# Turning 104 blocks of 128 by 128 on VectorE and by DMA instead of on TensorE, in a fused two-layer kernel on one core

## The chip, the core and the metric

The kernel runs on one core of one Trainium2 chip. The metric is the device time of one execution in microseconds (us), from the program's start to its end. TensorE (PE) multiplies matrices, VectorE (DVE) and ScalarE (ACT) work elementwise, GpSimd (POOL) does small jobs, SyncE (SP) issues almost all DMAs. PEld is TensorE's loading of the stationary operand.

## The reference, cut to what matters

Batch 1, 256 tokens, model width 2048, all in float32. Two layers follow each other.

```python
# layer 1 (first_block): proj = rms_norm(x) @ w_in          (10240 columns)
# differential attention on 4 heads, neighbourhood attention on 8 heads
mixed = g_a * (oa @ w_branch_a) + g_b * (on @ w_branch_b)
y = mixed @ w_out                       # x = x + rms_norm(y)
u = square(relu(rms_norm(x) @ w_up))    # x = x + rms_norm(u @ w_down)
# layer 2 (second_block): proj = rmsnorm(h) @ w_in_2
qk = silu(causal_dwconv(concat([ml_q, ml_k])))            # along the tokens
h_a = mlstm_chunkwise(q, k, v, i, f)
f_b = lb + (1 - lb) * sigmoid(hg_f); logf = log(f_b)      # cumulative sums along the tokens
h_b = hgrn2_chunkwise(q_b, k_b, logf, i_b)
h = h + concat([y_a, y_b]) @ w_out_2
gate = sigmoid(rmsnorm(h) @ w_pg_2);  h = h + gate * (p @ w_pe_2)
out = rmsnorm(h)
```

## The kernel before

Every large product runs as float32 split in two: a weight chunk of 512 rows by 512 columns (1 MB, four blocks of 128 rows) is loaded by SP into one of three `RAW` buffers, ACT rounds it into `HI` (`high`, L521), DVE subtracts to get `LO` (`low`, L936), and PE does three matmuls for each of the 4 row blocks and of the 2 token tiles, so 24 matmuls of 128x512 for a chunk. The activations, turned so that the contracted dimension lies on the partitions, are split in the same way into `ATH` and `ATL`.

There are 342 chunks, numbered by n in a list that every engine walks in the same order, with its own waits: 0 to 79 layer 1's `w_in`, 80 to 95 the two branches ("a", "b"), from `N_WO` = 96 `w_out`, from `N_UP` = 112 `w_up`, from `N_DN` = 176 `w_down`, from `N_IN2` = 240 layer 2's `w_in_2`, from `N_RES` = 308 `w_out_2` with `w_pe`, from `N_PG` = 326 `w_pg`. At step n ACT and DVE split chunk n+2, SP loads further ahead. `high(n)` waits until PE is done with chunk n-3, and SP's load of a chunk waits for DVE's `low` of the chunk three before it. Chunks 256 to 267 (the kind "nq") are narrower, 344 columns, so a step of PE is shorter there. Layer 2's `w_in_2` comes in the order hf (chunks 240 to 247), qk (248 to 255), nq (256 to 267), hv, vm, go, z, g.

The dictionary `side` (filled by `beside(n, name, ...)`) puts small steps behind the products of chunk n, in each engine's program: the convolution (`conv`, DVE), the forget gates (`prep`), the gate scans (`gate`), the attention steps (`da`, `na`), the recurrences (`hg`, `ml`). `behind[n]` and `before[n, t]` do this for the `unit` steps, which bring four turned blocks (group g of a product's input, token tile t) into `ATH` and `ATL`: "heads", "mix" (the gated sum `MX`), "r1", "r2", "y" and "pg" (the residual `XS` in front of `w_pg`).

Turning is done in two ways. (1) On PE: `tr` (L1478) is a matmul against the identity that gives a turned 128 by 128 block in PSUM; four of them are one step of `turned`. It serves `unit` (mix, r1, r2, y, pg), `to_heads` (layer 2's heads hf, qk, hq: PE turns 4 blocks for each token tile, ACT copies them from PSUM into `HB`, `QKR`, `HQ`), `ut` (the first up block) and the attention's `da turn`, `da back`, `na turn`. (2) On DVE and by DMA, used for the eight groups of layer 1's rope and hd heads: `turn(j)` (L1030) turns 128x512 in blocks of 32 by 32 for both token tiles; before the load of chunk m+6 (m is the step of the turn, in `turns_of`) SP waits for it and issues 8 DMAs of 64 KB from SBUF into a DRAM buffer `turned_rows[j]`, which put the blocks in their places; before the load of chunk m+7 SP waits until they have landed and loads the 512 KB back as heads ("heads", j).

Of the kernel before, what the change touches and what calls it, by code (L numbers as in the profile page):

```python
# [15 lines left out]
P = 128  # L16
D = 2048
S = 256
# [51 lines left out]
def program(nc, x, xt, w_in, w_a, w_b, w_out, w_up, w_down, w_in2, w_out2, w_pg, w_pe, p2,  # L70
            cols, lamv, rpb, rows, bif, cos_c, sin_c, nam_c, id_c, lvl_c, caus_c, out):
    with ExitStack() as ctx:
# [43 lines left out]
        def loaded(*name):  # L116
            if name not in s_ld:
                s_ld[name] = Count(sem("s_load_" + "_".join(map(str, name))), 16)
                counts.append(s_ld[name])
            return s_ld[name]  # L120
# [165 lines left out]
        for j, n in turns_of.items():  # L286
            beside(n, "turn", j)
# [9 lines left out]
        for t in range(2):  # L297
            beside(N_UP + 5 + t, "ut", 0, t)
        for j in range(1, 16):
            beside(N_UP + 4 * j + 4, "ut", j, 1)  # L300
        for i in range(3):
            beside(172 + i, "cut", i)
            beside(228 + i, "weigh", i)
        for j in range(2):
# [5 lines left out]
        for n, i in ((244, 0), (249, 1), (250, 2), (251, 3), (252, 4), (253, 5), (254, 6)):  # L310
            beside(n, "prep", i)
        for i in range(9):
            beside(257 + i, "conv", i)
# [3 lines left out]
        for i in range(3):  # L317
            beside(268 + i, "gate", i)
# [9 lines left out]
        beside(316, "p_parts")  # L328

# [9 lines left out]
        fill_early("mix", N_WO - 4, [(N_WO + 2, 1), (N_WO + 3, 0)])  # L339
        fill_early("y", N_RES - 4, [(N_RES + 2, 0), (N_RES + 2, 1)])  # L340
# [6 lines left out]
        def turned_to(j, t):  # L347

            return TURNED[(2 * (j if j < 4 else j - 2) + t) % 8]

        def heads_of(j):
            z = (QT, QT, KT, KT, None, None, QN, QN, KN, KN)[j]
            return z[:, 4 * (j % 2):4 * (j % 2) + 4, :]
# [10 lines left out]
        turned_rows = {j: nc.dram_tensor(f"turned{j}", (512, S), F32, kind="Internal").ap() for j in turns_of}  # L364
# [88 lines left out]
        def gpsimd(e):  # L453
# [15 lines left out]
            for n in range(N_ALL):  # L469
# [24 lines left out]
                if n == 266:  # L494
                    po.wait_ge(s_pe, "qk", 1, 1)
                    po.wait_ge(s_pool, LAST)
                    e.memset(VM[:, :, :, S:S + 1], 1.0).then_inc(s_pool.on("ones"))
# [6 lines left out]
        def scalar(e):  # L504
# [18 lines left out]
            def unit(name, g, t):  # L523
# [10 lines left out]
                elif name == "mix":  # L534
                    ac.wait_ge(s_pe, "unit", name, g, t)
                    ac.wait_ge(s_prod, "products", taken(name, g), t)
                    src = cut4(mis[:, place.get((name, g, t), 0), :])
# [10 lines left out]
            def cut(i):  # L548
                if i >= 64:
                    return  # L550
                ac.wait_ge(s_act, "ut", i % 16, 1)
# [3 lines left out]

            def to_heads(dst, g0, t, *name):
                ac.wait_ge(s_pe, *name)
                act(dst[:, g0:g0 + 4, t * P:(t + 1) * P], cut4(mis[:, place.get(name, 0), :]), ACT.Copy).then_inc(
                    s_act.on(*name))
# [65 lines left out]
            def ut(j, t):  # L625
                if j == 0:
                    ac.wait_ge(s_pe, "ut", 0, t)
                    act(UT[:, 0:4, t * P:(t + 1) * P], cut4(acc[:, 2 * (number["wo", 3] % 2) + t, :]), ACT.Square).then_inc(
                        s_act.on("ut", 0, t))
                else:  # L630
                    ac.wait_ge(s_dve, "up rows", j)
                    act(UT[:, 4 * j:4 * j + 4, :], UX[j % 2], ACT.Square).then_inc(s_act.on("ut", j, 1))
# [10 lines left out]
            def prep(i):  # L643
                if i == 0:
                    ac.wait_ge(s_dve, "lb")
                    act(ST[:, 16:32], ST[:, 16:32], ACT.Exp).then_inc(s_act.on("lb exp"))
                if i == 1:
                    ac.wait_ge(s_act, "hf", 1, 1)
                    act(HK, HB, ACT.Sigmoid, scale=-1.0).then_inc(s_act.on("hk"))
                if i == 2:  # L650
                    act(HB, HB, ACT.Sigmoid).then_inc(s_act.on("hb sig"))
                if i == 5:
                    ac.wait_ge(s_dve, "hb max")
                    act(HB, HB, ACT.Ln).then_inc(s_act.on("hb ln"))
# [85 lines left out]
            def evac(b):  # L740
# [6 lines left out]
                for t in range(2):  # L747
# [23 lines left out]
                    if kind == "up":  # L771
                        ac.wait_ge(s_pool, "r1")
                        act(US[:, t, :], ps[t], ACT.Relu, scale=ST[:, 52 + t:53 + t]).then_inc(s_act.on("evac", b, t))
                    if kind in ("nq", "hf", "qk", "hv", "vm", "go"):
                        ac.wait_ge(s_pool, "r2")
                    if kind == "nq":
                        act(NQ[:, t, 344 * j:344 * j + 344], ps[t], ACT.Copy, scale=RS[t]).then_inc(s_act.on("evac", b, t))
                    if kind == "hf":
                        if j:
                            ac.wait_ge(s_pe, "hf", 0, t)  # L780
# [3 lines left out]
                    if kind == "hv":  # L784
                        ac.wait_ge(s_pe, "qk", 1, 1)
                        act(HV[:, t, cols_], ps[t], ACT.Copy, scale=RS[t]).then_inc(s_act.on("evac", b, t))
                    if kind == "vm":
                        act(VM[:, t, 2 * j:2 * j + 2, 0:S], ps[t].rearrange("p (h c) -> p h c", h=2), ACT.Copy, scale=RS[t]).then_inc(s_act.on("evac", b, t))
                    if kind == "go":
                        ac.wait_ge(s_pe, "hq", 3)  # L790
# [50 lines left out]
            do = dict(lam=lam, da=da, na=na, sig=sig, ut=ut, rb=rb, cut=cut, prep=prep, conv=conv, gate=gate,  # L841
                      turn_v=turn_v, hg=hg, ml=ml, p_parts=p_parts)

            def beside_products(n):
                for name, *i in side.get(n, ()):
                    if name == "hf":
                        to_heads(HB, 4 * i[0], i[1], "hf", *i)
                    elif name == "qk":
                        to_heads(QKR, 4 * i[0], i[1], "qk", *i)
                    elif name == "hq":  # L850
                        to_heads(HQ, 4 * (i[0] // 2), i[0] % 2, "hq", *i)
                    elif name in do:
# [56 lines left out]
        def vector(e):  # L909
# [38 lines left out]
            def unit(name, g, t):  # L948
                if name in SCALE:
                    z = cut4(stage(name, g, t))  # L950
                    c0 = SCALE[name] + 4 * g
                    dv.wait_ge(s_pe, "unit", name, g, t)
                    dv.wait_ge(loaded("col"), "col")
                    tt(z, cut4(mis[:, place.get((name, g, t), 0), :]),
                       COL[:, c0:c0 + 4].unsqueeze(2).broadcast_to([P, 4, P]), ALU.mult).then_inc(s_dve.on("unit", name, g, t))

            def unit_low(name, g, t):
# [3 lines left out]
                elif name == "mix":  # L961
                    src = cut4(mis[:, place.get((name, g, t), 0), :])
# [58 lines left out]
            def turn(j):  # L1021
                if j == 0:
                    dv.wait_ge(s_pe, "x sums")
                if j >= 6:
                    dv.wait_ge(loaded("blocks", j - 6), "blocks", j - 6)
                for t in range(2):
                    if j >= 6:
                        dv.wait_ge(s_act, "evac", number["hd", j], t)
                    then()
                    e.transpose(turned_to(j, t), R[t]).then_inc(s_dve.on("turned", j, t))  # L1030
# [35 lines left out]
            def prep(i):  # L1066
                if i == 0:
                    a0, a1 = COL[:, C_LB:C_LB + 8], COL[:, C_LB + 8:C_LB + 16]
                    dv.wait_ge(loaded("col"), "col")
                    tt(LB, a0, a1, ALU.max).then_inc(s_dve.on())  # L1070
                    tt(LM, a1, LB, ALU.subtract).then_inc(s_dve.on())
                    tt(LB, a0, LB, ALU.subtract).then_inc(s_dve.on("lb"))
                    dv.wait_ge(s_act, "lb exp")
                    tt(LM, LB, LM, ALU.add).then_inc(s_dve.on())
                    then()
                    e.reciprocal(LM, LM).then_inc(s_dve.on())
                    tt(LB, LB, LM, ALU.mult).then_inc(s_dve.on())
                    ts(LM, LB, -1.0, 1.0, ALU.mult, ALU.add).then_inc(s_dve.on())
                if i in (3, 4):
                    dv.wait_ge(s_act, "hb sig")  # L1080
                    for h in range(4 * (i - 3), 4 * (i - 3) + 4):
                        ts(HB[:, h, :], HB[:, h, :], LM[:, h:h + 1], LB[:, h:h + 1], ALU.mult, ALU.add).then_inc(s_dve.on())
                        ts(HK[:, h, :], HK[:, h, :], LM[:, h:h + 1], None, ALU.mult).then_inc(s_dve.on())
                if i == 5:
                    ts(HB, HB, 1e-19, None, ALU.max).then_inc(s_dve.on("hb max"))
                if i == 6:
                    dv.wait_ge(s_act, "hb ln")
                    for h in range(8):
# [3 lines left out]
            def conv(i):  # L1092
                if i < 8:
                    x_, y_ = QKR[:, i, :], QK[:, i, :]
                    cw = lambda k: COL[:, C_CW + 8 * k + i:C_CW + 8 * k + i + 1]
                    dv.wait_ge(s_act, "qk", 1, 1)
# [32 lines left out]
            def hg(q, i):  # L1129
# [57 lines left out]
                if i == 1:  # L1187
                    dv.wait_ge(s_act, "hg edge", q)
                    tt(HP[:, :, 0:P], HW_[:, :, 0:P], k_[:, :, 0:P], ALU.mult).then_inc(s_dve.on())
                    dv.wait_ge(s_act, "hq", 3)  # L1190
# [209 lines left out]
            do = dict(lam=lam, turn=turn, da=da, na=na, cut=cut, weigh=weigh, prep=prep, conv=conv, gate=gate, hg=hg, ml_logs=ml_logs, ml=ml, ya=ya,  # L1400
# [70 lines left out]
        def tensor(e):  # L1471
# [30 lines left out]
            def unit(name, g, t):  # L1502
                if name in ("heads", "x"):
# [51 lines left out]
            def columns(n):  # L1555
# [6 lines left out]
                if k == 0:  # L1562
# [3 lines left out]
                    elif block == 2:  # L1566
                        for t in range(2):
                            pe.wait_ge(s_act, "ut", 0, t)
# [29 lines left out]

            def ut(j, t):
                if j:  # L1600
                    return
                z = acc[:, 2 * (number["wo", 3] % 2) + t, :]
                pe.wait_ge(s_act, "rb")
                pe.wait_ge(s_dve, "evac", number["wo", 3], t)
                pe.wait_ge(s_act, "evac", number["up", 0], t)
                for c in range(4):
                    r = tr(z[:, c * P:(c + 1) * P], US[:, t, c * P:(c + 1) * P])
                r.then_inc(s_pe.on("ut", 0, t))
# [27 lines left out]
            def da(u):  # L1636
# [13 lines left out]
                if 0 <= u - 1 < 8:  # L1650
# [273 lines left out]
```

## Time and profile before

| | us |
|---|---|
| median of 3 runs | 1970.18 (1970.17 to 1970.8) |
| the profiled execution's own time | 1971.09 |
| its span, first to last instruction | 1969.1 |
| granted TensorE clock over the span | 0.999 |

A page shows one execution. Its parts used here are the busy time of each engine, the chain of work that ended last, the groups of instructions by line, the DMA issues, and the views of instructions in order of time. PE's busy time has modelled ends: a matmul's own duration overlaps that of the next, so what a matmul adds to the time is read from starts, not from durations.

### The profile page before, as it was taken

The page shows a single profiled execution, that of the slowest core. Times are in us where ns is not written, and L with a number is a line of the kernel's source. Part 1 is how long each engine was busy: PE and PEld are TensorE (multiplying, and loading weights), DVE is VectorE, ACT ScalarE, POOL GpSimd, SP SyncE. Part 2 cuts the span into 40 slices and gives each one's busy share as a digit, 9 for nine tenths or more (in the row PEclk, how much of TensorE's full clock was granted, in tenths as well). Part 3 has the DMA queues.
Part 4 walks back from the last instruction along what each step waited for, and adds up shares of the span by engine and source line. Part 5 has one row for each costly group of instructions (what it writes and reads, how often), then busy time and mean ns, then how long its engine had stood idle before and what let it go on. Part 6 is the DMA issues. An engine that isn't in the chain of part 4 may idle for free.

```text
span 1969.1 us, 22753 instructions
## 1 busy us (share of the span) xinstructions
PE 1956.4 (99%) x9394; PEld 1642.9 (83%) x9394; DVE 1225.9 (62%) x1172; ACT 979.4 (50%) x940; POOL 19.8 (1%) x31
## 2 busy tenths in 40 slices
PE   9999999999999999999999999999999999999998
PEld 7888888888888888888888888888889888888886
DVE  7846546645666644555566666677567768676565
ACT  6345535545445444444455555565555546544444
POOL 0000000000000000000000000000000000000000
PEclk9999999999999999999999999999999999999999
DMA  9874765565648356666555555565546544555463
GB/s 317 255 226 150 227 211 182 174 221 193 216 170 275 108 178 194 186 191 192 174 193 195 195 195 195 195 215 198 171 145 200 171 158 163 179 174 199 170 214 107
DMA packets 224215, 377.63 MB, mean 192 GB/s; under 512 B 40940, under 2 KB 52336, under 8 KB 223472
## 3 DMA queue, kind: packets, MB, share of 16 engines
q1 hardware_dynamic: 223096, 374.60, 58.0%
q8 instruction: 74, 1.21, 0.3%
q10 hardware_dynamic: 1016, 1.59, 0.2%
q14 instruction: 29, 0.24, 0.0%
HBM read 369.86 MB, written 6.30 MB: 191 GB/s over the span
## 4 chain that ended last, share of the span: by engine, by line
PE 90%; DVE 4%; issue 2%; ACT 2%; DMA 1%; POOL 0%; SPq 0%; POOLq 0%; DVEq 0%; ACTq 0%
PE acc L1475 77%; PE mis L1475 12%; PE mis L1478 1%; ACT hi L521 1%; DVE m L918 1%; DVE lo L936 1%; DMA raw<-in_w_in 1%; DVE m L926 1%; ACT m L510 0%; POOL st L459 0%; ACT m L511 0%; DVE lo L946 0%; DVE xs L1030 0%; DVE st L1011 0%; DVE at L940 0%
## 5 line engine op out<-in xcount | busy, mean ns | idle before, releaser
L1475 PE MATMUL acc<-hi,at 128*128 128x512 f32 (+1 forms) x4384 | 1363.2, 389 | 0.7 <-DVE lo L936 0.7
L936 DVE TENSOR_TENSOR lo<-raw,hi 128x2048 fp32r<-128x2048 f32 (+1 forms) x333 | 753.6, 2266 | 544.0 <-ACT hi L521 542.2
L1475 PEld LDWEIGHTS acc<-hi,at 128*128 128x128 f32 x4384 | 819.8, 188 | 165.5 <-DVE lo L936 1.7
L521 ACT ACTIVATE hi<-raw 128x2048 fp32r<-128x2048 f32 (+1 forms) x333 | 628.8, 1891 | 477.9 <-PE acc L1475 412.5
L1475 PE MATMUL acc<-lo,at 128*128 128x512 f32 (+1 forms) x2192 | 845.8, 386 | 0.0
L1475 PEld LDWEIGHTS acc<-lo,at 128*128 128x128 f32 x2192 | 411.7, 188 | 80.3 <-DVE lo L946 0.6
L1475 PE MATMUL mis<-at,hi 128*128 128x512 f32 x512 | 139.7, 394 | 0.0
L1475 PE MATMUL acc<-at,hi 128*128 128x512 f32 x448 | 122.2, 394 | 0.0
L1475 PEld LDWEIGHTS mis<-at,hi 128*128 128x128 f32 x512 | 88.0, 189 | 12.4
L918 DVE TENSOR_TENSOR m<-m 128x256 f32<-128x256 f32 (+1 forms) x145 | 75.1, 518 | 21.6 <-ACT m L510 17.1
L1475 PEld LDWEIGHTS acc<-at,hi 128*128 128x128 f32 x448 | 77.0, 189 | 10.9
L1475 PEld LDWEIGHTS mis<-at,lo 128*128 128x128 f32 x512 | 77.4, 189 | 10.0
L510 ACT ACTIVATE m<-acc,st 128x512 f32<-128x512 f32 (+2 forms) x74 | 49.1, 664 | 66.5 <-PE acc L1475 65.7
L510 ACT ACTIVATE m<-mis 128x256 f32<-128x256 f32 (+2 forms) x57 | 30.4, 534 | 104.0 <-PE mis L1475 57.2
L1475 PE MATMUL mis<-at,lo 128*128 128x256 f32 x512 | 80.6, 281 | 0.0
L973 DVE TENSOR_TENSOR at<-m,at 128x1024 fp32r<-128x1024 f32 x64 | 78.0, 1220 | 4.0 <-ACT at L553 4.0
L510 ACT ACTIVATE m<-m 128x1024 f32<-128x1024 f32 (+4 forms) x51 | 53.2, 1043 | 54.1 <-DVE m L918 37.9
L1475 PEld LDWEIGHTS acc<-at,lo 128*128 128x128 f32 x448 | 67.8, 189 | 8.9
L1475 PE MATMUL mis<-m 128*128 128x128 f32 (+3 forms) x384 | 72.5, 324 | 0.5 <-DVE m L918 0.5
L1475 PE MATMUL acc<-at,lo 128*128 128x256 f32 x448 | 70.1, 281 | 0.0
L553 ACT ACTIVATE at<-m 128x1024 fp32r<-128x1024 f32 x64 | 66.7, 1042 | 6.5 <-PE mis L1475 6.5
L1475 PEld LDWEIGHTS mis<-m 128*128 128x128 f32 x384 | 56.4, 190 | 7.8 <-DVE m L918 2.0
(133 smaller groups left out, 722.3 us busy)
## 6 DMA issues: line engine op xcount, KB each, us to landing
raw<-in_w_in SPq DMA_DIRECT2D x133, 1024.0 KB, 5.1
raw<-in_w_up SPq DMA_DIRECT2D x64, 1024.0 KB, 5.4
raw<-in_w_down SPq DMA_DIRECT2D x64, 1024.0 KB, 5.1
raw<-in_w_out SPq DMA_DIRECT2D x32, 1024.0 KB, 5.1
raw<-in_w_pg SPq DMA_DIRECT2D x16, 1024.0 KB, 5.1
raw<-in_w_in SPq DMA_DIRECT2D x12, 688.0 KB, 4.3
raw<-in_w_a SPq DMA_DIRECT2D x8, 1024.0 KB, 5.1
raw<-in_w_b SPq DMA_DIRECT2D x8, 1024.0 KB, 5.0
```

The source lines that it names most:

```text
L510: return e.activation(o, i, f, scale=scale, bias=bias)
L521: e.activation(hi_of(n), raw_of(n), ACT.Copy).then_inc(s_hi.on("hi", n))
L553: e.activation(ATH[:, 4 * (i % 4):4 * (i % 4) + 4, :], UT[:, 4 * (i % 16):4 * (i % 16) + 4, :], ACT.Copy).then_inc(s_ach.on("cut hi", i))
L918: return e.tensor_tensor(o, a, b, op)
L926: return e.scalar_tensor_tensor(o, a, s, b, op0, op1)
L936: e.tensor_tensor(lo, raw, hi.bitcast(F32), ALU.subtract).then_inc(s_lo.on("lo", n))
L973: e.tensor_tensor(ATL[:, s4:s4 + 4, :], UT[:, k:k + 4, :], ATH[:, s4:s4 + 4, :].bitcast(F32), ALU.subtract).then_inc(s_dve.on("cut", i))
L1475: return e.matmul(o, a, b, start=start, stop=stop)
L1478: return e.transpose(o, a, IDN[:, :])
```

## The change

`unit` no longer turns on PE the groups 0 to 2 of "mix" and of "pg"; `to_heads` and `ut`'s PE part are gone. In their place 13 turns of kind (2) are added: hf 0 and 1 (steps 244, 248), qk 0 and 1 (252, 256), hq 0 and 1 (264, 268), mix 0 to 2 (84, 88, 92), ut 0 (117), pg 0 to 2 (312, 316, 320). Group 3 of mix and of pg stays on PE. Readers of the turned data wait for ("heads", ...) and read SBUF instead of PSUM.

Around this: `prep` is split into `bounds` (step 244) and `forget(j, i)`, which does one half of the heads at a time; `conv` 0 to 7 moves from steps 257 to 264 to steps 256 to 263 and `conv` 8 stays at 265; `gate` 2 moves from step 270 to 271; the units (mix, 2) move from step 94 to 95; the square of the first up block is done before the turn, as a second ACT instruction for each tile; in `da(u)` PE's transposes "da turn" come after the scores instead of before them.

The core of the diff:

```diff
-        for j, n in turns_of.items():
-            beside(n, "turn", j)
+        turns_of.update({("hf", 0): 244, ("hf", 1): 248, ("qk", 0): 252, ("qk", 1): 256, ("hq", 0): 264, ("hq", 1): 268})
...
-        for t in range(2):
-            beside(N_UP + 5 + t, "ut", 0, t)
...
-        for j in range(2):
-            for t in range(2):
-                beside(244 + 4 * j + t, "hf", j, t)
-                beside(252 + 4 * j + t, "qk", j, t)
-        for i in range(4):
-            beside(268 + i, "hq", i)
...
+        for j in range(2):
+            beside(247 + 4 * j, "forget", j, 0)
+            beside(249 + 4 * j, "forget", j, 1)
+            beside(250 + 4 * j, "forget", j, 2)
+            beside(251 + 4 * j, "forget", j, 3)
...
+        turns_of.update({("mix", g): N_AB + 4 * g + 4 for g in range(3)})
+        turns_of[("ut", 0)] = N_UP + 5
+        turns_of.update({("pg", g): N_RES + 4 * g + 4 for g in range(3)})
...
+        behind[N_WO - 1] = behind.pop(N_WO - 2)
...
             def unit(name, g, t):
-                if name in ("heads", "x"):
+                if name in ("heads", "x") or name in ("mix", "pg") and g < 3:
                     return
...
-            def to_heads(src, b, t, *name):
-                pe.wait_ge(s_act, "evac", b, t)
-                turned(name, lambda c: src[:, c * P:(c + 1) * P], name, 4, s_act, *name)
```

VectorE in the narrow chunks, before: the splits of chunks 257 to 262 and the first two convolutions (`m<-m,col`).

```order
L1090 SCALAR_TENSOR_TENSOR m<-rst,m 128x256 x8
L936 TENSOR_TENSOR lo<-raw,hi 128x1376 x3
L922 TENSOR_SCALAR m<-m,col 128x256
L926 SCALAR_TENSOR_TENSOR m<-m,col 128x255
L926 SCALAR_TENSOR_TENSOR m<-m,col 128x254
L926 SCALAR_TENSOR_TENSOR m<-m,col 128x253
L936 TENSOR_TENSOR lo<-raw,hi 128x1376
```

And in the changed kernel, in the same place:

```order
L1118 SCALAR_TENSOR_TENSOR m<-rst,m 128x256 x4
L940 TENSOR_TENSOR lo<-raw,hi 128x1376
L926 TENSOR_SCALAR m<-m,col 128x256
L930 SCALAR_TENSOR_TENSOR m<-m,col 128x255
L930 SCALAR_TENSOR_TENSOR m<-m,col 128x254
L930 SCALAR_TENSOR_TENSOR m<-m,col 128x253
L1055 STREAM_TRANSPOSE m<-m 128x512 x2
L940 TENSOR_TENSOR lo<-raw,hi 128x1376
```

The convolutions begin three splits earlier, and the two block transposes of qk 1 stand behind the first of them.

SP from the last of layer 2's wide hf and qk loads on, before:

```order
L379 DMA raw<-in_w_in 128x4x512 x14
L379 DMA raw<-in_w_in 128x4x344 x4
L374 DMA m<-in_idn 128x128
L379 DMA raw<-in_w_in 128x4x344 x8
L379 DMA raw<-in_w_in 128x4x512 x40
```

And in the changed kernel, the part of it around the narrow chunks:

```order
L389 DMA raw<-in_w_in 128x4x344 x2
L384 DMA turned<-m 32x16x32 x8
L389 DMA raw<-in_w_in 128x4x344
L384 DMA m<-turned 128x4x256
L389 DMA raw<-in_w_in 128x4x344
L384 DMA m<-in_idn 128x128
L389 DMA raw<-in_w_in 128x4x344 x2
L384 DMA turned<-m 32x16x32 x8
L389 DMA raw<-in_w_in 128x4x344
L384 DMA m<-turned 128x4x256
```

Each turn puts 8 block DMAs and one load of heads between the loads of weights, here those of qk 0 and qk 1.

PE behind chunk 268, before (four transposes for hq 0, then the gates' four small products):

```order
L1475 MATMUL acc<-hi,at 128x512
L1478 MATMUL mis<-idn,m 128x128 x4
L1475 MATMUL mis<-idn,m 4x128 x4
L1475 MATMUL acc<-hi,at 128x512
L1475 MATMUL acc<-lo,at 128x512
```

And in the changed kernel:

```order
L1503 MATMUL acc<-hi,at 128x512
L1503 MATMUL mis<-idn,m 4x128 x4
L1503 MATMUL acc<-hi,at 128x512
L1503 MATMUL acc<-lo,at 128x512
```

The transposes between two chunks are gone, the small products stay.

## Rows read from the trace of the kernel before

**Rows 1.** The page's busy time of each engine.
```profile
PE 1956.4 (99%) x9394; PEld 1642.9 (83%) x9394; DVE 1225.9 (62%) x1172; ACT 979.4 (50%) x940; POOL 19.8 (1%) x31
```

**Rows 2.** The page's chain that ended last, shares by engine.
```profile
PE 90%; DVE 4%; issue 2%; ACT 2%; DMA 1%; POOL 0%; SPq 0%; POOLq 0%; DVEq 0%; ACTq 0%
```

**Rows 3.** The chain in order of time, layer 1's products: start us, us, what.
```profile
216.62 76.21 PE acc L1475 x336
...
409.81 141.49 PE acc L1475 x624
551.30 0.88 PE mis L1478 x8
...
557.64 0.87 PE mis L1478 x8
```

**Rows 4.** The chain in order of time, at layer 2's heads and the up blocks.
```profile
1400.97 0.44 PE mis L1478 x4
...
1406.89 0.44 PE mis L1478 x4
...
1467.47 0.44 PE mis L1478 x4
...
1471.67 0.44 PE mis L1478 x4
...
701.52 0.44 PE acc L1478 x4
...
707.55 22.43 PE acc L1475 x128
```

**Rows 5.** The view of line 1478: duration in ns, min/median/max.
```profile
L1478 PE MATMUL mis<-idn,m x160: 270/272/330, 149.4 to 1783.9; 128*128 128x128 f32 x160
```

**Rows 6.** The view of line 1030, the block transposes on DVE: ns min/median/max.
```profile
L1030 DVE STREAM_TRANSPOSE xs<-m x16: 702/710/715, 49.0 to 249.5; 128x512 f32<-128x512 f32 x16
```

**Rows 7.** SP's instructions in order of time, one turn of layer 1: start, us.
```profile
227.62 6.17 SPq L374 DMA_DIRECT2D turned<-xs  x8
...
235.35 0.38 SPq L374 DMA_DIRECT2D m<-turned  x1
```

**Rows 8.** The page's DMA issues: count, KB each, median us from issue to landing.
```profile
raw<-in_w_in SPq DMA_DIRECT2D x12, 688.0 KB, 4.3
...
turned<-xs SPq DMA_DIRECT2D x64, 64.0 KB, 2.9
m<-turned SPq DMA_DIRECT2D x8, 512.0 KB, 6.0
```

**Rows 9.** DVE in order of time, two splits in the narrow chunks.
```profile
1474.67 1.58 DVE L936 TENSOR_TENSOR lo<-raw,hi 128x1376 fp32r<-128x1376 f32 x1
...
1478.06 1.58 DVE L936 TENSOR_TENSOR lo<-raw,hi 128x1376 fp32r<-128x1376 f32 x1
```

**Rows 10.** ACT in order of time, two roundings there, each waiting for PE.
```profile
1483.43 1.36 ACT L521 ACTIVATE hi<-raw 128x1376 fp32r<-128x1376 f32 x1 [1.96 <-PE acc L1475]
1487.19 1.36 ACT L521 ACTIVATE hi<-raw 128x1376 fp32r<-128x1376 f32 x1 [2.40 <-PE acc L1475]
```

**Rows 11.** Behind them: ACT at the gates, DVE's low part of chunk 272, PE's start of it.
```profile
1519.09 0.42 ACT L510 ACTIVATE m<-m 4x256 f32<-4x256 f32 x1 [2.82 <-DVE m L926]
1519.53 1.28 ACT L510 ACT_TABLE_LOAD   x1
...
1521.14 1.90 ACT L521 ACTIVATE hi<-raw 128x2048 fp32r<-128x2048 f32 x1
...
1530.16 2.29 DVE L936 TENSOR_TENSOR lo<-raw,hi 128x2048 fp32r<-128x2048 f32 x1 [2.59 <-ACT hi L521]
...
1535.72 5.47 PE acc L1475 x24
```

**Rows 12.** The differential attention: what PE's transposes waited for, and two splits on DVE.
```profile
PE mis L1478 <- DVE m L926: 0.7, 2, 0.4
...
180.62 2.29 DVE L936 TENSOR_TENSOR lo<-raw,hi 128x2048 fp32r<-128x2048 f32 x1 [0.53 <-ACT hi L521]
...
188.33 2.29 DVE L936 TENSOR_TENSOR lo<-raw,hi 128x2048 fp32r<-128x2048 f32 x1 [0.53 <-ACT hi L521]
```

More of the change, by code:

```diff
@@ L316, in program @@
         beside(266, "hg", 0, 0)
-        for i in range(3):
-            beside(268 + i, "gate", i)
+        for i, n in enumerate((268, 269, 271)):
+            beside(n, "gate", i)
         for i in range(1, 13):
@@ L328, in program @@
         beside(316, "p_parts")
+        turns_of.update({("mix", g): N_AB + 4 * g + 4 for g in range(3)})
+        turns_of[("ut", 0)] = N_UP + 5
+        turns_of.update({("pg", g): N_RES + 4 * g + 4 for g in range(3)})
+        for j, n in turns_of.items():
+            beside(n, "turn", j)
         before, behind = {}, {}
@@ L534, in unit @@
                 elif name == "mix":
-                    ac.wait_ge(s_pe, "unit", name, g, t)
+                    if g < 3:
+                        ac.wait_ge(loaded("heads", (name, g)), "heads", (name, g))
+                        src = heads_of((name, g))[:, :, t * P:(t + 1) * P]
+                    else:
+                        ac.wait_ge(s_pe, "unit", name, g, t)
+                        src = cut4(mis[:, place.get((name, g, t), 0), :])
                     ac.wait_ge(s_prod, "products", taken(name, g), t)
-                    src = cut4(mis[:, place.get((name, g, t), 0), :])
                 else:
@@ L625, in ut @@
             def ut(j, t):
[L626 to L632, printed above, removed]
+                ac.wait_ge(s_dve, "up rows", j)
+                act(UT[:, 4 * j:4 * j + 4, :], UX[j % 2], ACT.Square).then_inc(s_act.on("ut", j, 1))
             def rb():
@@ L1064, in weigh, with bounds @@
                     tt(o, o, NB[:, 512 * j:512 * j + 512], ALU.mult).then_inc(s_dve.on("weighed row", j, t))
[L1066 to L1081, printed above, removed]
+            def bounds():
+                a0, a1 = COL[:, C_LB:C_LB + 8], COL[:, C_LB + 8:C_LB + 16]
+                dv.wait_ge(loaded("col"), "col")
+                tt(LB, a0, a1, ALU.max).then_inc(s_dve.on())
+                tt(LM, a1, LB, ALU.subtract).then_inc(s_dve.on())
+                tt(LB, a0, LB, ALU.subtract).then_inc(s_dve.on("lb"))
+                dv.wait_ge(s_act, "lb exp")
+                tt(LM, LB, LM, ALU.add).then_inc(s_dve.on())
+                then()
+                e.reciprocal(LM, LM).then_inc(s_dve.on())
+                tt(LB, LB, LM, ALU.mult).then_inc(s_dve.on())
+                ts(LM, LB, -1.0, 1.0, ALU.mult, ALU.add).then_inc(s_dve.on())
@@ L1086, in prep @@
[L1086 to L1088 removed]
+                if i == 2:
+                    hb = HB[:, 4 * j:4 * j + 4, :]
+                    ts(hb, hb, 1e-19, None, ALU.max).then_inc(s_dve.on("hb max", j))
+                if i == 3:
+                    dv.wait_ge(s_act, "hb ln", j)
+                    for h in hs:
                         then()
@@ L1398, in finish @@
                         ts(o, o if c == 2 else SG[t], r, None, ALU.mult).then_inc(s_dve.on("out", t, c))
-            do = dict(lam=lam, turn=turn, da=da, na=na, cut=cut, weigh=weigh, prep=prep, conv=conv, gate=gate, hg=hg, ml_logs=ml_logs, ml=ml, ya=ya,
+            do = dict(lam=lam, turn=turn, da=da, na=na, cut=cut, weigh=weigh, bounds=bounds, forget=forget, conv=conv, gate=gate, hg=hg, ml_logs=ml_logs, ml=ml, ya=ya,
                       p_parts=p_parts)
@@ L1566, in columns @@
                     elif block == 2:
-                        for t in range(2):
-                            pe.wait_ge(s_act, "ut", 0, t)
+                        pe.wait_ge(s_act, "rb")
                     else:
```

154 lines of the change are left out of this document (81 added, 73 removed).

## The prediction

> **What bounds the kernel now.** I read the busy times first. PE is busy 1956.4 us, 99% of the span of 1969.1; DVE 62%, ACT 50% [rows 1]. The chain that ended last agrees: 90% of it is PE [rows 2]. The granted clock is 0.999 over the whole span, the upper of its two levels, so nothing is to be gained or lost there unless PE starts to wait long. Then the chain in order of time shows a pitch: 624 matmuls, which are 26 chunks of 24, take 141.49 us [rows 3], so 5.44 us for a chunk of three-product work; four up chunks take 22.43 us [rows 4], 5.61 each; a narrow chunk is the distance of two roundings on ACT that each wait for PE, 1487.19 - 1483.43 = 3.76 us [rows 10]. What PE does less comes off the time one for one, as long as the split chunks keep coming in time. So there are two questions: what a transpose on PE adds to this pitch, and whether ACT, DVE or SP become late somewhere.
>
> **PE's transposes removed.** 104 go: 24 of mix, 24 of pg, 8 of the first up block, 16 each of hf, qk and hq. Their duration is 272 ns [rows 5], but matmuls overlap, so I take starts. In layer 1's products eight transposes stand between chunks, which then start 557.64 - 551.30 = 6.34 us apart [rows 3]. Against 5.44 a group of eight adds 0.90 us. A group of four adds 1406.89 - 1400.97 - 5.44 = 0.48 [rows 4]; in the narrow chunks 1471.67 - 1467.47 - 3.76 = 0.44 [rows 4, 10]; in the up chunks 701.52 + 0.44 + 5.59 = 707.55 against a pitch of 5.61, so 0.44 [rows 4]. The sum: mix 3 x 0.90 and pg 3 x 0.90 = 5.40; hf and hq 4 groups each and qk 0 two, 10 x 0.48 = 4.80; qk 1 2 x 0.44 = 0.88; the first up block 2 x 0.44 = 0.88. Together **12.0 us**, 0.115 us for a transpose.
>
> The Trainium skill (TensorE: Matmul & The Clock Gate, Part 4) gives a PE transpose of this size about 275 ns in a kernel's context. That is this trace's duration of 272 ns [rows 5], and 104 of them would be an estimate of 28.6 us. The starts say 0.11 to 0.12, and starts set the sum.
>
> **VectorE's transposes added.** 26 instructions of 128x512 at 0.71 us [rows 6] = 18.5 us on DVE, 1.43 us for a turn. DVE has 743 us free over the span, so in the wide regions this is covered: a wide step of 5.44 us holds a split of 2.29 [rows 11] and the turn, with 1.7 us left. ACT loses the copies out of PSUM, gains two squares and, since the forget gates run in halves, some switches of its function table at 1.28 us [rows 11]. Those steps (247 to 255) are wide ones where ACT does one rounding of 1.90 [rows 11] per 5.44: nothing on the path.
>
> **DMAs and SP's queue.** Each turn puts 8 block DMAs, 6.17 us of issuing, into SP between two weight loads; its heads load goes out 235.35 - 227.62 = 7.7 us after the first block [rows 7], and lands 6.0 later [rows 8]: a round trip of 13.7 us. Layer 1 already has eight such turns beside 5.44-us chunks, and two of them stand inside the unbroken piece of 14 chunks, 336 matmuls in 76.21 us from 216.62 on [rows 3], again 5.44 each. So a turn beside wide chunks is worth nothing either way. That covers mix, ut, hf, qk 0, and pg. Readers of mix, ut and pg heads stand 3 or more steps (over 16 us) behind the turn, which is longer than the 13.7 of the round trip.
>
> **The narrow chunks are the place that is not covered.** Per step of 3.76 us DVE has a split and a convolution, which recur at 1478.06 - 1474.67 = 3.39 us [rows 9]: 0.37 us to spare, while the turns of qk 1 (step 256) and hq 0 (264) add 1.43 each. The convolutions move ahead by three splits, which frees DVE later but adds to its start. On SP, the turn of qk 1 stands ahead of the weights of chunk 262, and its heads load ahead of chunk 263. By my estimate the heads load goes out at about 1475.7 (evacuation of the last qk chunk, one split, one convolution of 0.41 + 1.52, two transposes, then 7.7). The 0.69 MB of chunk 263 alone lands 4.3 us after issue [rows 8]; behind a heads load of 6.0, between 1480.4 and 1486. I take 1484. Then rounding (1.36 [rows 10]) and split (1.58 [rows 9]) end at 1486.9. PE wants the chunk at 1487.19 + 3.76 [rows 10], less the 3.8 saved so far (hf 1.92, qk 1.84): 1487.1. So it is just in time. The following chunks have 0.4 to 1.6 us by the same reckoning.
>
> The next tight place is the gates. Before, the low part of chunk 272 was ready at 1530.16 + 2.29 = 1532.45 and PE came at 1535.72 [rows 11], 3.3 us later. Now PE comes 5.7 us earlier (3.8 and hq's 1.9), while the ping-pong of ACT and DVE for the gates (0.42, table 1.28, 0.42, rounding 1.90, split 2.29 [rows 11]) moves forward less, by about 2 to 3 us: it follows PE's small products of chunk 268, and one gate step is put off by a chunk. That makes 0 to 1 us of waiting. For both places I take a stall of **0.5 us**. Its bounds: 0, if the loads overlap well, and 4 us, if one turn's round trip is exposed (13.7 against three narrow steps, 11.3, is 2.4) and the gates wait their full 1. Half a microsecond since the worked-out times meet within 0.4.
>
> **The rest.** In the differential attention the turn of a unit now follows the next scores. PE's transposes there waited 0.7 us in total [rows 12]. But the steps recur at 188.33 - 180.62 = 7.71 us, longer than a chunk, and are paced by splits that wait for ACT and not by PE [rows 12]. I take 0; between 0.7 gained and 1 lost. Removing a wait of PE there moves it to the split.
>
> **Sum.** -12.0 + 0.5 + 0 = -11.5 us. The profiled execution (own time 1971.09, 0.9 above the median) goes to about 1959.6, its span from 1969.1 to 1957.6; the median from 1970.18 to **1958.7**.
>
> **Rivals.**
> (A) VectorE and SP set the pace through the narrow chunks. For it: 0.37 us of room per step [rows 9], two turns of 1.43 and their 16 block DMAs in some 12 steps. Against: ACT still waits 2.40 us for PE in every step there [rows 10], so the split is a buffer or two ahead. 2 x 1.43 with a load or two late by 2 to 3 us gives 3 to 8 us of stall: 1961.2 to 1966.2.
>
> The Trainium skill (DMA: Bandwidth & Descriptors, Specifications) wants 512 bytes or more in a piece of a transfer for full rate; the blocks move in pieces of 128. Here 64 KB of such pieces land in 2.9 us [rows 8], beside weights that go on arriving in layer 1. If these pieces slow the weights, it is A that grows.
>
> (B) Slower than before. Every turn's 6.17 us of issuing on SP comes onto the weights' path. In layer 1 the loads are three chunks ahead; they are not if the three `RAW` buffers come free late, which they do where ACT's rounding is at once followed by the load's need. The point from which it decides: a weight chunk that lands after ACT is free to round it. Then hf 1, qk 0, qk 1, hq 0 and hq 1 each cost 6.17, 31 us, less 12: +19, 1989. Against it: layer 1's turns cost PE nothing. The Trainium skill (VectorE: DVE Perf Modes, the three transpose paths) also speaks against the change: it sends a 128 by 128 turn to TensorE when the result may lie in PSUM. By the rows that would be right only in this case, since PE is the full engine.
>
> (C) A transpose is worth its own duration: 104 x 0.272 = 28.3 us, 1942. The pitch in [rows 3] speaks against it; only a hidden loss around each group could bring it.
>
> (D) The gain is eaten: the heads arrive late in two or three of the regions, each time a round trip less the room for it, and the result is within 4 us of before.
>
> **How the numbers follow.** The forecast case (stall up to 2.5 us, 1956.8 to 1961) gets 0.68, A 0.21, D 0.05, B 0.03, C 0.03. The range of 8 in 10 takes the forecast case and most of A: 1956.8, that is, a gain of 12.0 with da's 0.7 and some room for a transpose at 0.12, up to 1965.0. A measurement of this kernel tells 0.2%, 3.9 us, from no change. All of A to 1966.2 and the forecast case are faster by more than that: 0.92; same 0.05; slower 0.03.
>
> **What the changed profile would show.** PE's busy time down by 12 us and its line of transposes at 64 instead of 160 in `mis`; chunks 80 to 95 in one unbroken piece at 5.44 but for group 3. In the narrow chunks the distance of two roundings on ACT: 3.76 if I am right, above 4 in some steps with A, and there the rounding would wait for the weights' load instead of PE. PE's wait for a low part near chunk 272, under 1 us. Steps of 7.7 us in the attention as before. It would be wrong if PE waits for heads in layer 2 (hf's forget gates late, hence the recurrence), if DVE's splits wait for landed blocks, or if the pitch of the chunks between 240 and 268 is above 5.44 and 3.76.

## The result, and the profile of the changed kernel

The changed kernel takes 1958.34 us (median of 4, 1958.19 to 1959.11) against 1970.18 before; the ratio is 0.9939 with an interval of 0.9925 to 0.9953. That is 11.8 us less, where 11.5 were forecast, and 1958.34 where 1958.7 was; in the later pair of medians below, 1970.62 and 1958.36, it is 12.3 us less. The profiled execution took 1958.19 us, its span is 1956.3, at a granted clock of 0.998.

The page of the changed kernel, busy time, its chain's shares, and its DMA issues (count, KB each, median us from issue to landing), which answer to [rows 1, 2, 8]:

```profile
PE 1943.7 (99%) x9290; PEld 1632.3 (83%) x9290; DVE 1242.2 (63%) x1199; ACT 977.2 (50%) x933; POOL 17.8 (1%) x31
...
PE 90%; DVE 4%; ACT 3%; issue 3%; POOL 0%; ACTq 0%; POOLq 0%; DVEq 0%
...
m<-turned SPq DMA_DIRECT2D x21, 512.0 KB, 5.7
raw<-in_w_in SPq DMA_DIRECT2D x12, 688.0 KB, 5.3
```

PE has 104 instructions and 12.7 us less and is still 99% of the span. DVE has 16.3 us more, and its share of the chain is 4% as before. The loads of the narrow chunks land in 5.3 us instead of 4.3; below it is shown who waits for them, and that PE does not.

The chain in order of time, changed kernel (start us, us, what), to be held against [rows 3, 4]:

```profile
214.93 76.21 PE acc L1503 x336
...
408.12 171.41 PE acc L1503 x756
...
685.44 16.84 PE mis L1503 x96
...
1379.34 126.81 PE acc L1503 x648
```

Where three groups of eight transposes cut layer 1's products, one piece now runs from chunk 67 into chunk 98. The three chunks of 32 behind chunk 116 take 16.84 us in one piece, 5.61 each, where the first up block's transposes stood before [rows 4]. Layer 2's hf, qk and narrow chunks, which eight groups of four cut up before [rows 4], are one piece of 126.81 us. The piece of 336 matmuls is 76.21 us long in both kernels [rows 3].

For a finer account I worked out each chunk's period, the time between the ends of PE's last products of neighbouring chunks, from the semaphore events in the two traces, and summed it over stretches. No view prints these periods:

| chunks | what changed in them | before, us | after, us | gained |
|---|---|---|---|---|
| 2 to 24 | nothing meant | 126.39 | 125.65 | 0.74 |
| 25 to 35 | attention: order on PE, DVE's turn | 78.92 | 78.25 | 0.67 |
| 36 to 80 | | 263.91 | 263.91 | 0.00 |
| 81 to 112 | mix | 189.63 | 186.91 | 2.72 |
| 113 to 128 | first up block | 82.39 | 81.55 | 0.84 |
| 129 to 240 | | 629.33 | 629.32 | 0.01 |
| 241 to 256 | hf, qk 0 | 80.10 | 77.19 | 2.91 |
| 257 to 268 | qk 1, narrow chunks | 47.73 | 46.85 | 0.88 |
| 269 to 276 | hq, gates | 52.26 | 50.48 | 1.78 |
| 277 to 320 | | 273.88 | 273.87 | 0.01 |
| 321 to 328 | pg | 47.16 | 45.41 | 1.75 |
| 329 to 338 | | 54.40 | 54.40 | 0.00 |

The turned stretches give 2.72 + 0.84 + 2.91 + 0.88 + 1.78 + 1.75 = 10.88 us. Two gains are not PE's transposes, 0.67 and 0.74, and some 0.5 lies ahead of chunk 2 and behind the last products, in two single executions. In the changed kernel each chunk from 244 to 255 has a period of 5.44, each from 256 to 267 one of 3.76 (256: 3.75): PE waits for nothing there.

### The profile page after: what moved, and what is told of

The parts are those of the page before. It is cut to its first block, busy times and chain, and to the rows that moved or that the text cites. A ratio compares the mean times of both kernels' runs of the same rounds, so it can differ in the third digit from the quotient of the medians.

```text
span 1956.3 us, 22685 instructions
## 1 busy us (share of the span) xinstructions
PE 1943.7 (99%) x9290; PEld 1632.3 (83%) x9290; DVE 1242.2 (63%) x1199; ACT 977.2 (50%) x933; POOL 17.8 (1%) x31
## 4 chain that ended last, share of the span: by engine, by line
PE 90%; DVE 4%; ACT 3%; issue 3%; POOL 0%; ACTq 0%; POOLq 0%; DVEq 0%
PE acc L1503 78%; PE mis L1503 12%; ACT hi L531 1%; DVE m L922 1%; DVE lo L940 1%; PE mis L1506 1%; DVE m L930 1%; ACT m L520 0%; ACT m L521 0%; ACT at L556 0%; DVE at L974 0%; DVE st L1019 0%; POOL st L469 0%; DVE st L926 0%; DVE sm L926 0%
## 5 line engine op out<-in xcount | busy, mean ns | idle before, releaser
L556 ACT ACTIVATE at<-m 128x512 fp32r<-128x512 f32 x46 | 28.9, 632 | 77.8 <-DVE m L922 64.4
L520 ACT ACTIVATE m<-mis 128x256 f32<-128x256 f32 (+2 forms) x45 | 23.3, 517 | 84.2 <-PE mis L1503 59.1
```

The costliest lines, as they stand in the source:

```text
L520: return e.activation(o, i, f, scale=scale, bias=bias)
L556: e.activation(h, src, ACT.Copy).then_inc(s_ach.on("ath", name, g, t))
```

## Experiments

The stretches repeat between kernels to 0.05 us, while medians of one kernel differ by some tenths. So I read the small effects from the periods, and give the medians beside them. The changed kernel was run again as a base.

> The changed kernel itself on the chip of the other runs of this call, as their base: 1958.3 to 1958.9. What its executions differ by, some 0.7 us, is to my reading GpSimd's first power (the root of the first norm), which took 2.7 us in the profiled executions of before, e2, e3, e5 and e8 and 0.7 in those of the changed kernel, e1, e4, e6 and e7, and moves chunk 10's period between 6.1 and 5.47: single executions should lie about 1958.2 or about 1958.9.

Measured: 1958.36 (1958.13 to 1958.97, 5 runs). Its periods are those of the table to 0.06.

**The price of a transpose.** In the kernel before, each of 96 transposes twice:

```diff
-                for c in range(n):
-                    r = tr(mis[:, i, c * P:(c + 1) * P], src(c))
+                more = name[0] in ("hf", "qk", "hq") or name[0] in ("mix", "pg") and name[1] < 3
+                for c in range(2 * n if more else n):
+                    r = tr(mis[:, i, c % n * P:(c % n + 1) * P], src(c % n))
```

> The kernel before, with 96 of the 104 transposes (mix and pg groups 0 to 2, hf, qk, hq; not the first up block) done twice on PE into the same place. Theory 1 (a transpose adds its start pitch of 0.115 us where PE is the bound): + 96 x 0.115 = 11.0 us, 1981.2. Rival C (a transpose is worth its duration of 0.272): + 26.1, 1996.3. Below 11 if PE's added time lets the splits catch up somewhere (the waits at chunk 272 or at pg become smaller): not under + 9.

Measured: 1981.19 (ratio to before 1.0052, 1.0038 to 1.0065), 10.6 us above the 1970.56 of before beside it. The chain of it in order of time:

```profile
551.25 1.75 PE mis L1478 x16
552.99 5.46 PE acc L1475 x24
558.46 1.75 PE mis L1478 x16
```

Sixteen take 1.75 where eight took 0.88 [rows 3]. By periods the stretches of the table rose by 2.62, 2.55, 0.89, 1.72 and 2.62, 10.4 us for 96. So a further transpose costs 0.108 us, and the 272 ns of [rows 5] overlap with what stands around it; C, which needed 26, is out.

**Layer 2's heads back on PE.** All of hf, qk, hq and the steps of `prep`, `conv` and `gate` as before; mix, first up block and pg stay turned by DVE.

```diff
-        turns_of.update({("hf", 0): 244, ("hf", 1): 248, ("qk", 0): 252, ("qk", 1): 256, ("hq", 0): 264, ("hq", 1): 268})
+        for j in range(2):
+            for t in range(2):
+                beside(244 + 4 * j + t, "hf", j, t)
+                beside(252 + 4 * j + t, "qk", j, t)
+        for i in range(4):
+            beside(268 + i, "hq", i)
```

> The changed kernel with layer 2's heads hf, qk and hq as before: 48 transposes on PE, ACT's copies, the gates' and convolutions' old steps, no turns there. Theory 1 (48 transposes at their pitch, 5.68 us, and the turns cost nothing in the narrow chunks): 1958.6 + 5.6 = 1964.2. Rival A in a weak form (the turns take a part back, waits at chunks 269 to 272 and in the narrow chunks): the difference is smaller, 3 to 5 us, 1961.6 to 1963.6.

Measured: 1964.27 (0.9968, 0.9956 to 0.998), 5.9 above the base; by periods the three stretches are 80.10, 47.73 and 52.26, exactly those of before: 5.57 in all, where theory 1 had 5.6 and e3's second set of the same transposes cost 5.16. Theory 1 holds: the six turns took nothing back, as the unbroken periods of 5.44 and 3.76 also show.

**Why nothing was lost in the narrow chunks.** ACT in the changed kernel (start us, us, operation, then in brackets its idle time and what ended it), beside SP's and DVE's instructions in the same place:

```profile
1463.10 1.36 ACT L531 ACTIVATE hi<-raw 128x1376 fp32r<-128x1376 f32 x1 [2.40 <-PE acc L1503]
1466.86 1.35 ACT L531 ACTIVATE hi<-raw 128x1376 fp32r<-128x1376 f32 x1 [2.40 <-PE acc L1503]
...
1471.56 1.36 ACT L531 ACTIVATE hi<-raw 128x1376 fp32r<-128x1376 f32 x1 [0.39 <-DMA raw<-in_w_in]
1474.99 1.36 ACT L531 ACTIVATE hi<-raw 128x1376 fp32r<-128x1376 f32 x1 [2.08 <-DMA raw<-in_w_in]
```
```profile
1462.44 4.09 SPq L384 DMA_DIRECT2D turned<-m  x8
1466.57 0.52 SPq L389 DMA_DIRECT2D raw<-in_w_in  x1
1467.98 0.38 SPq L384 DMA_DIRECT2D m<-turned  x1
1468.40 21.07 SPq L389 DMA_DIRECT2D raw<-in_w_in  x7
```
```profile
1461.70 1.53 DVE L1055 STREAM_TRANSPOSE m<-m 128x512 f32<-128x512 f32 x2
1463.15 1.55 DVE L940 TENSOR_TENSOR lo<-raw,hi 128x1376 fp32r<-128x1376 f32 x1
```

Two roundings, of chunks 262 and 263, do wait for their weights instead of for PE. That is the mechanism that I had named. To hold the times against the prediction's, its clock must be shifted: it took off what hf and qk save, 3.8 us, but not what is saved ahead of them. PE ended chunk 262 at 1490.9 before and at 1481.9 now, so the prediction's times stand 5.2 us late, and its 1475.7 for the heads load is 1470.5 here. The load went out at 1467.98, 2.5 us ahead of that. The first block went out at 1462.44 where the prediction has 1462.8, so nearly all of it is SP: the eight DMAs were issued in 4.09 us and not in 6.17. Chunk 263's weights landed at about 1474.9, 6.9 us behind the heads load's issue and not 8.3. Its low part was ready 3.6 us ahead of PE, where my reckoning had 0.2.

The 6.17 of [rows 7] was one turn out of eight; the first two in the same trace took 4.13 and 4.15, the fourth 7.39.

How far the room reaches, two kernels show. First, twice as many block DMAs of half the size, so the same bytes:

```diff
-                                load(z[:, :, k], turned_to(j, t)[i, :].rearrange("p (c k) -> p c k", c=16), "blocks", j)
+                                for c in (slice(0, 8), slice(8, 16)):
+                                    load(z[:, c, k], turned_to(j, t)[i, :].rearrange("p (c k) -> p c k", c=16)[:, c, :], "blocks", j)
```

> The changed kernel with 16 block DMAs of 32 KB for a turn instead of 8 of 64 KB (the same bytes in the same pieces of 128 bytes), for all 21 turns: SP issues for about 12.2 us where it issued for 6.1. Theory 1 (issuing is hidden until a weight load lands behind ACT's need; there are 3 to 5 us of room in layer 2's heads and more in the wide chunks): 1 to 3 us of waiting beside the turns of layer 2's heads, nothing elsewhere, 1958.3 to 1962. Rival B (what SP issues lies on the weights' path): 21 x 6.1 = 128 us, 2086. In between, if only the turns of hf, qk and hq are exposed: 6 x 3 to 6 us = 18 to 36, 1977 to 1994.

Measured: 1965.95 (10 runs), 7.6 above the base. Its narrow turn and PE's waits for the low parts:

```profile
1466.27 7.74 SPq L384 DMA_DIRECT2D turned<-m  x16
...
PE acc L1504 <- DVE lo L941: 4.4, 7, 1.4
```

By periods: chunks 262 and 263 + 2.0, 271 and 272 + 1.2, 275 to 280 + 1.5, and in layer 1 chunks 13 and 14 + 2.1, behind the two turns of steps 6 and 7. Chunk 10 has 0.8 more for another reason (below). The issuing of the 21 turns, first block to last, rose from 120 us to 179, so by 59 and not by the 128 expected: doubling the count doubled it only where it had been short. For these 59 us PE lost 6.7 by periods. So rival B's mechanism exists, but it costs in four places and nothing at most turns. My 1 to 3 us were too few: layer 2 lost 4.6, and I had not looked at layer 1's start. Beside qk 1, 7.74 us of issuing instead of 4.09 used up the room and cost 2.0.

Second, DVE's turning doubled:

```diff
                     then()
+                    e.transpose(turned_to(j, t), src).then_inc(s_dve.on())
+                    then()
                     e.transpose(turned_to(j, t), src).then_inc(s_dve.on("turned", j, t))
```

> The changed kernel with each of DVE's block transposes done twice into the same place: 1.43 us more for a turn, 30 us more of DVE in all. Theory 1 (DVE has room even in the narrow chunks, where the splits end 2.1 to 4.5 us ahead of PE): 1958.3 to 1959.3, the narrow chunks stay at 3.76. Rival A (the narrow chunks are DVE's): up to 2 x 1.43 = 2.9 more and 1.4 at chunk 28 of the attention, 1961 to 1963.

Measured: 1968.50 (10 runs), 10.1 above the base. The waits of PE in it (us in total, times, longest):

```profile
PE acc L1505 <- DVE lo L940: 5.2, 4, 2.7
PE mis L1508 <- DVE m L930: 1.5, 2, 1.3
```

By periods: chunk 10 + 4.6 (steps 6 and 7 again), chunks 31 and 33 + 1.4, chunk 259 + 2.2, chunks 271, 272 and 325 + 1.2. Rival A's costs came nearly as it had them: 2.16 at chunk 259 and 0.81 at 271 and 272 against 2.9, 1.40 in the attention against 1.4. Neither theory had chunk 10, the largest. Its low part is ready 0.35 us ahead of PE in the profile of the changed kernel, and 0.31 us late in that of the kernel before, which has the slow power of GpSimd (below); so there is hardly room for more on DVE. Chunk 259, behind two doubled turns, had a low part with 2.1 us of room in the changed kernel. Rival A is thus right about what would bind: turns of twice the length are no longer hidden. The 1.43 us of a turn fit. But 6.0 us of the loss belong to layer 1's eight turns, which both kernels have; at the 13 added ones it is 3.4.

**The 0.67 us in the attention.** The change puts PE's transposes behind the scores; I had taken this at 0. First, that order undone:

> The changed kernel with one part undone: in the differential attention PE's transposes of unit u-1 stand ahead of the scores of unit u again. Theory 1 (PE sets the pace there, and the old order made it wait for DVE's result): the chunks 26 to 34 take about 0.7 us longer, 59.0 instead of 58.3 us for the nine, the time is 1958.3 + 0.7 = 1959.0, and PE's waits of its transposes for DVE come back as 0.7 in 2 times. Theory 2 (what the prediction said: ACT and DVE set the pace there and the order is worth nothing): unchanged, 1958.3, steps of 7.65 us.

Measured: 1958.84, chunks 25 to 35 in 78.19. Chunk 30 stays at 7.65. So the order on PE is worth nothing, and still the 0.67 is real. What is left of the change in this place stands only in the order on DVE: all turns are now entered behind the other small steps, layer 1's as well. Before (first row) and after (second row), DVE in order of time:

```profile
173.55 1.45 DVE L1030 STREAM_TRANSPOSE xs<-m 128x512 f32<-128x512 f32 x2
176.69 0.69 DVE L1011 TENSOR_REDUCE st<-mis 128x2 f32<-128x512 f32 x1
```
```profile
174.14 0.69 DVE L1019 TENSOR_REDUCE st<-mis 128x2 f32<-128x512 f32 x1
177.65 1.46 DVE L1055 STREAM_TRANSPOSE xs<-m 128x512 f32<-128x512 f32 x2
```

The turn of chunk 28 stood ahead of the softmax's maximum, and stands behind it now. Two kernels put it in front again, with either order on PE:

```diff
+        for j, n in turns_of.items():
+            beside(n, "turn", j)
         turns_of.update({("hf", 0): 244, ("hf", 1): 248, ("qk", 0): 252, ("qk", 1): 256, ("hq", 0): 264, ("hq", 1): 268})
...
         for j, n in turns_of.items():
-            beside(n, "turn", j)
+            if isinstance(j, tuple):
+                beside(n, "turn", j)
```

> The changed kernel with one unspoken part of it undone: DVE's eight block transposes of layer 1 stand again ahead of the other small steps of their chunk (the changed kernel writes all turns behind them; at chunk 28 this puts 1.45 us of turning ahead of the softmax of the differential attention). The new order of PE (scores, then transposes) stays. Theory 1 (DVE's place of the turn cost PE its wait at chunk 30, and the scores that now stand ahead, 1.03 us, cover it): chunk 30's period 7.66, time as the changed kernel, 1958.3 to 1958.8. Theory 2 (the turn alone decides, whatever PE's order): chunk 30 at 8.1, the nine chunks 26 to 34 at 58.9 instead of 58.2, 1959.0 to 1959.5.

> As e7_turn_first, and with PE's transposes ahead of the scores too, so that both parts are as before in layer 1. Theory 1 and 2: chunk 30's period 8.1, the nine chunks 58.9, 0.7 more than the changed kernel: 1959.0 to 1959.5. If the nine chunks stay at 58.2, the 0.7 came neither from the turn's place nor from the order.

Measured: 1959.17 and 1959.72. Chunks 25 to 35 take 78.96 and 78.91, in both about 0.7 more than the changed kernel. PE's waits of its transposes, new order and then old:

```profile
PE mis L1509 <- DVE m L933: 1.0, 1, 1.0
```
```profile
PE mis L1509 <- DVE m L933: 0.7, 2, 0.4
```

With the new order chunk 30 is indeed free of its wait (7.66), but chunk 33 has 0.6 more: covered in one place, paid in the next. Theory 2 holds in the sum, not at chunk 30. The 0.67 us are DVE's order. (The nine chunks of these expectations take 66.2 us in the changed kernel and 66.9 before; their 58.2 to 59.0 are no sums of nine periods, the difference of 0.7 is right.)

**The 0.95 us missing at pg.** Three groups of eight are worth 2.70, the stretch gained 1.75. The pg groups back on PE:

```diff
-        turns_of.update({("pg", g): N_RES + 4 * g + 4 for g in range(3)})
...
-                    if name == "pg" and g < 3:
+                    if False:
...
-                if name in ("heads", "x") or name in ("mix", "pg") and g < 3:
+                if name in ("heads", "x") or name == "mix" and g < 3:
```

> The changed kernel with the three pg groups turned on PE again. Theory 1 (the trace after: at chunk 325 PE has caught up with the alternation of ACT and DVE, which takes 7.5 us a step, and gives back 0.87 of the 2.70 saved): 1958.3 + 1.85 = 1960.2, and chunk 325's period falls from 7.21 to about 6.35 while 322 to 324 rise from 5.44 to 6.34. Theory 2 (the full pitch of three groups of eight comes back): 1958.3 + 2.7 = 1961.0. Theory 3 (removing pg's transposes bought nothing there): 1958.3.

Measured: 1960.75, 2.4 above the base by medians, 47.16 against 45.41 by periods. The periods of 322 to 325 are 6.34, 6.36, 6.33 and 6.37, in the changed kernel 5.44, 5.44, 5.44 and 7.21. By the periods theory 1 holds; the medians alone could not tell 1.85 from 2.7. ACT in the changed kernel there:

```profile
1831.04 1.91 ACT L531 ACTIVATE hi<-raw 128x2048 fp32r<-128x2048 f32 x1
1835.91 0.63 ACT L556 ACTIVATE at<-m 128x512 fp32r<-128x512 f32 x1 [2.96 <-DVE m L922]
1838.03 0.63 ACT L556 ACTIVATE at<-m 128x512 fp32r<-128x512 f32 x1 [1.49 <-DVE m L922]
1838.56 1.90 ACT L531 ACTIVATE hi<-raw 128x2048 fp32r<-128x2048 f32 x1
```

ACT waits for DVE twice in a step, and DVE, behind its split, for ACT: a round of 1838.56 - 1831.04 = 7.52 us a step, against PE's 5.44. In the kernel before the round was as long, 7.58 from chunk 324's rounding to chunk 325's, but PE took 6.34 a step. The low parts' lead over PE falls from 6.1 us at chunk 323 to 2.0 at 325, and the last group's steps, which queue on DVE and ACT behind this round, come late for PE. Doing both multiplications ahead of both low parts shortens the round:

```diff
+                if len(us) == 2 and us[0][0] in SCALE:
+                    for u in us:
+                        unit(*u)
+                    for u in us:
+                        unit_low(*u)
```

(the loop ahead of it skips these).

> The changed kernel with another order of DVE at the y and pg units: both multiplications of a group (t = 0 and 1) and then both low parts, so that ACT's second high part does not wait for the first low part. Theory 1 (the alternation ACT rounding 1.81, DVE split 2.17, multiplication, ACT's part, low part, multiplication, ACT's part, 7.5 us a step, is what PE meets at chunk 310, period 6.94 against 5.44, and at 325, 7.21 against 6.34): a step of the alternation falls to about 6.8, both waits shrink or go, 1.5 + 0.9 = 2.4 us at most, 1956.0. Theory 2 (the waits there come from the evacuations, not from the alternation): 1958.3, and the two periods stay.

ACT in that kernel:

```profile
1830.66 1.91 ACT L531 ACTIVATE hi<-raw 128x2048 fp32r<-128x2048 f32 x1
1835.52 1.36 ACT L556 ACTIVATE at<-m 128x512 fp32r<-128x512 f32 x2 [2.96 <-DVE m L922]
1836.79 1.90 ACT L531 ACTIVATE hi<-raw 128x2048 fp32r<-128x2048 f32 x1
```

Measured: 1956.80 (0.9931, 0.9918 to 0.9943), 1.6 below the base. The round is 6.13 us. Chunk 325 falls from 7.21 to 6.33, 326 from 5.56 to 5.44, and 310, where the y units alternate in the same way, from 6.93 to 6.38: 1.5 us. What is left of the two, 6.33 and 6.38, is the pitch of 5.44 and eight transposes at 0.9, so both waits are gone. The 2.4 us of theory 1 counted the y group's transposes as waiting. This is the fastest kernel here.

**The 0.74 us ahead of chunk 24.** They stand in chunk 10, 6.11 before and 5.47 after (the rest in chunk 6). GpSimd's first power, kernel before and then changed kernel:

```profile
40.70 2.70 POOL L459 TENSOR_TENSOR st<-st,mhalf 128x2 f32<-128x2 f32 x1 [39.16 <-DVE st L922]
```
```profile
39.82 0.71 POOL L469 TENSOR_TENSOR st<-st,mhalf 128x2 f32<-128x2 f32 x1 [38.27 <-DVE st L926]
```

In all profiled executions chunk 10 was at 6.1 to 6.2 when this operation took about 2.7 us (before, e2, e3, e5, e8) and at 5.47 when it took 0.7 (changed, again, e1, e4, e7, e9, e10; e6 has its own delay there). The kernels of the two sets do not differ in what GpSimd does up to there, so I count the 0.74 as a difference of executions and not of the change. That the operation is what delays chunk 10 rests on this pairing and on chunk 10's missing room; no run changed it alone. The five executions of the changed kernel above fall in two groups, 1958.13 to 1958.36 and 1958.88 to 1958.97, as expected, but only one of them has a profile. One attempt at its cause gave GpSimd a power to do at the start:

```diff
             e.memset(ONE[:, :], 1.0).then_inc(s_pool.on("one 1"))
+            po.wait_ge(s_pool, LAST)
+            e.tensor_tensor(ONE[:, 0:1], ONE[:, 0:1], MHALF[:, 0:1], ALU.pow).then_inc(s_pool.on("one"))
```

> e4_units_in_pairs and one more edit: GpSimd does one power on a 128x1 constant at the start (1 to the -1/2, which leaves it 1), before its first real power at chunk 5. Theory 1 (the first power of an execution is sometimes 2 us slower, from something that belongs to first use): chunk 10 at 5.47 in every execution, 1956.7 with a spread of 0.2 instead of 0.7 to 0.9. Theory 2 (the 2 us are not from first use): spread and median as e4, 1956.6 to 1957.5.

Measured: 1957.15 (1956.63 to 1957.65, 5 runs). The spread stays at 1.0 us, so theory 2: first use is not what makes an execution longer, or this edit does not cure it. What does is open.

## Why the prediction was right, and where its steps were not

**The bound and the sum: right.** PE's pitch carried the time. By the table, mix was sized at 2.70 and gave 2.72, the first up block 0.88 and 0.84, hf and qk 0 at 2.88 and gave 2.91, qk 1 0.88 and 0.88, hq 1.92 and 1.78, since its groups stand beside the gates' small products and cost 0.40 to 0.47 each there instead of 0.48. e3 and e10 show that this is the price of the transposes themselves. The count in the forecast for the profile was a slip: the row of `mis<-idn,m` goes from 160 to 88, since pg's transposes stand under `xs`.

**pg: 2.70 became 1.75.** The step that failed is "a turn beside wide chunks is worth nothing either way. That covers mix, ut, hf, qk 0, and pg", with the readers of pg taken as far enough behind. They were; the heads came in time. But I did not ask what is late next once PE goes faster there: the alternation of ACT and DVE at 7.5 us a step, which in the kernel before already cost PE a wait of some 0.6 us at chunk 310, with the y units. e2 and e4 show it.

**The stall of 0.5 us: not there.** The heads load was put 2.5 us too late in the changed kernel's clock, since the issuing was taken from a single turn, and the landing of the weights behind it 1.4 us too long. The room for chunks 262 to 265 was 3.3 to 4.4 us, not 0.2 to 1.6. The periods and e10 leave no room for a stall. At the gates the estimate was nearer. DVE's low part of chunk 272 in the changed kernel, then PE's chain there, as against [rows 11]:

```profile
1521.18 4.50 DVE L940 TENSOR_TENSOR lo<-raw,hi 128x2048 fp32r<-128x2048 f32 x2 [2.60 <-ACT hi L531]
```
```profile
1523.70 0.98 PE mis L1503 x8
1524.68 5.69 PE acc L1503 x24
```

The first half of the DVE row ends at 1523.47. PE ended chunk 271 at 1523.7, did the gates' eight small products and began chunk 272 at 1524.7 without a wait: 1.2 us of room, where it was 3.3 before. I had 0 to 1 us of waiting.

**The attention: 0, and 0.67 came.** The value for the order on PE was right (e1), its reason was not: the low parts were ready 4 us ahead of PE there, so PE's own work of 7.65 us a step set the pace, and not the splits. And DVE's new place of layer 1's turns was in the diff, whose first two lines take them out of where they stood, and I did not weigh it.

**So the 11.5 us were met by parts that cancel:** 0.95 too much at pg and 0.1 at hq, against 0.5 of a stall and 0.67 of DVE's order that I did not have. That gives 11.6 for the change; the medians say 11.8 to 12.3. That the forecast of 11.5 came so near is luck in this part: the sum of the transposes was right, the corrections to it were not.

**The rivals.** C fell with e3. B and A are mechanisms that e5 and e6 could bring out, with twice the block DMAs and twice the turning, 7.6 and 10.1 us, in part at layer 1's old turns. D, heads that arrive late, did not come about: in the changed kernel ACT waited for a heads load twice, 1.1 and 0.4 us, and no stretch of the table grew. The Trainium skill's preference for TensorE when the result may lie in PSUM (VectorE: DVE Perf Modes, Rules for kernel authors) does not hold in this kernel, by 1958.36 against 1964.27 for layer 2's heads alone.

## What to carry to other kernels

What an instruction adds to a full engine is read from the starts of its neighbours, with it and without it, never from its own duration; here the two differ by 2.5 times, 272 ns against 108. Where an engine is made faster, write down for each stretch the round of the other engines, and how much it has in hand at the start: the gain stops where that is used up. And compare the order of every queue between the two kernels, also for steps that were not meant to move; this one moved 0.67 us. And take a time that varies, as SP's issuing does, from all its rows and not from one.

## What the runs showed of the hardware

- A transpose of 128x128 float32 on PE lasts 270 to 272 ns in its row and adds 0.11 us to a full PE, eight 0.88, sixteen 1.75.
- Eight DMAs of 64 KB in pieces of 128 bytes took SP 4.09 to 7.76 us to issue over the 21 turns of the changed kernel, sixteen of 32 KB 7.73 to 10.01 (e5). The shortest is 0.51 and 0.48 us for one, so there the time goes by their number and not by bytes; what lengthens the others is open.
- Beside these turns the narrow chunks' loads of 688 KB landed in 5.3 us (median) instead of 4.3.
- GpSimd's first power of a norm took 0.7 us in some executions and 2.7 to 2.8 in others, and with it chunk 10's period went from 5.4 to 5.5 to 6.1 to 6.2. The cause is open.
